# Delta rule of a hybrid block: a symmetric decay table, beta applied as the triangle leaves PSUM, key scaling in front of the weight splits, and the inverse turned over

## The chip, the cores and the metric

The kernel runs on one core of one Trainium2 chip. The metric is the device time of one execution in microseconds; lower is better. Engines are called by their names in the profile: PE is TensorE (PEld its weight loads), DVE VectorE, ACT ScalarE, POOL GpSimd, SP SyncE, which only issues transfers here. Each engine works through its own list of instructions in order, and engines wait for each other by semaphores.

## The reference

Two transformer-like blocks over 512 tokens of width 1024. The change lies in one branch of the first block, a gated delta rule with 8 heads, keys of 128 and values of 256 columns. Everything is float32.

```python
qa = l2norm(qa) * (A_DK ** -0.5)
ka = l2norm(ka)
beta = jax.nn.sigmoid(beta_logit)
g = -jnp.exp(a_log) * jax.nn.softplus(a_dt + dt_bias)
...
g_cum = jnp.cumsum(g, axis=-1)                      # within a chunk
decay = jnp.exp(jnp.where(causal, g_cum[..., :, None] - g_cum[..., None, :], -jnp.inf))
k_beta = k * beta[..., None]
lower = jnp.where(strict, jnp.einsum('bhncd,bhnmd->bhncm', k_beta, k) * decay, 0.0)
t_inv = triangular_solve(lower, eye, unit_diagonal=True)
u = t_inv @ (v * beta)
w = t_inv @ (k_beta * exp(g_cum))
attn = jnp.where(causal, jnp.einsum('bhncd,bhnmd->bhncm', q, k) * decay, 0.0)
# then chunk by chunk, with a state of 128 x 256 per head:
# v_new = u - w @ state;  o = (q * exp(g_cum)) @ state + attn @ v_new;  state = state * last_dec + k_dec.T @ v_new
```

The kernel takes chunks of 128 tokens, not of 64, which is the same function. All else of both blocks (projections, a retention branch, attention of three kinds, 16 experts) is as before.

## The kernel before

The program is written out by hand, one list per engine. A semaphore object (`Sig`) gives each step a name: `c_pe.mark(ins, "KK0.1")` counts it up, `dve.wait_ge(*c_pe("KK0.1"))` waits for it. In names, `j` is the head within a pair and `p` the pair; four pairs follow each other (`chain_a(p)`, p = 0 to 3, on every engine).

Between the steps of a pair lie weight matmuls of the projections that later pairs need. A generator `gemm` gives them in steps: one step is three matmuls of 128x512, the two-part product of `product` (L93, L94, L95), 8 steps a group, 12 groups a pair. `fill(n)` emits n of them at fixed places, with numbers from the table `FILL` (`root` 8, `scores` 6, `turn` 6, `inverse` 4, `level` 3 and 3, ...). On ScalarE and VectorE the same `fill` emits what belongs to a group that has ended: the eviction of its bank (L797), the high part of a later weight piece (L82 on ScalarE), its low part (L87 on VectorE), and the convolution of the next pair (L808, L1918, L812). A weight piece is split four groups ahead of use. SyncE loads 2 MB of weights when the group that read the slot last has ended.

The steps of a pair, in TensorE's order, with the lines of the profile:

1. Sums of squares of queries and keys by a matmul with ones (L1317 into `bank_a`, L1318 into `bank_b`, head by head), behind the scaling of the previous pair's output (L2031) that reads `bank_a`.
2. ScalarE makes 1/norm of them: a logarithm (L851), a table load, an exponential (L856, "root"), and then the exponential of the decay table D (L859), which VectorE has laid out (L1952). Then it does its `fill(root)`.
3. VectorE does its own `fill(root)` (one weight split, L87) and then scales keys (L1958) and queries (L1961).
4. GpSimd multiplies the scaled keys by beta (L590, `kbT`), masks D to a triangle (L593), and makes the queries for the state (L598, `qeT`).
5. TensorE does 8 steps of weights, then KK = keys by beta-keys (L1324) and KQ = keys by queries (L1329). VectorE multiplies both by D as they leave PSUM (L1965 into `LT`, L1968 into `ATT`).
6. After 6 steps, keys and values are transposed (L1334, L1344); GpSimd masks `LT` with the mask of level 0 (L609).
7. The inverse of I + L by 7 levels of doubling blocks. Per level: GpSimd masks (`NM`, L609), TensorE multiplies by X (L1359), ScalarE copies (L873), TensorE makes the updates of X and Y (L1367, L1370), VectorE adds them (L1997, L2000). X is the inverse and Y its transpose, weight steps lie between.
8. The recurrence over the four chunks (L1385 to L1402), norms, transposes of the output (L1410), and its scaling (L2031).

## Time and profile before

| | us |
|---|---|
| median of 3 runs | 2854.88 |
| lowest, highest | 2853.36, 2857.54 |
| the profiled execution | 2853.58 |
| its span in the profile | 2851.9 |
| PE busy | 2582.3 (91%) |
| DVE busy | 1122.2 (39%) |
| ACT busy | 833.4 (29%) |
| POOL busy | 250.7 (9%) |

The span is the time between the first and the last instruction of one execution. Busy shares are averages over the whole program. The four pairs of the delta rule lie between about 86 and 650 us of the span. A row of the timeline gives start, duration, engine, line, operation and how many instructions were merged into it; in brackets is how long the engine had stood idle and whose instruction ended that. A float32 matmul shows as two records, so 16 records are 8 products. A matmul's duration includes its way through the array, so consecutive ones overlap: work is read from starts.

### The profile page before, as it was taken

The page shows a single profiled execution, that of the slowest core. Times are in us where ns is not written, and L with a number is a line of the kernel's source. Part 1 is how long each engine was busy: PE and PEld are TensorE (multiplying, and loading weights), DVE is VectorE, ACT ScalarE, POOL GpSimd, SP SyncE. Part 2 cuts the span into 40 slices and gives each one's busy share as a digit, 9 for nine tenths or more (in the row PEclk, how much of TensorE's full clock was granted, in tenths as well). Part 3 has the DMA queues.
Part 4 walks back from the last instruction along what each step waited for, and adds up shares of the span by engine and source line. Part 5 has one row for each costly group of instructions (what it writes and reads, how often), then busy time and mean ns, then how long its engine had stood idle before and what let it go on. Part 6 is the DMA issues. An engine that isn't in the chain of part 4 may idle for free.

```text
span 2851.9 us, 30016 instructions
## 1 busy us (share of the span) xinstructions
PE 2582.3 (91%) x12308; PEld 1928.0 (68%) x12308; DVE 1122.2 (39%) x1539; ACT 833.4 (29%) x1327; POOL 250.7 (9%) x240
## 2 busy tenths in 40 slices
PE   6898989899999899988999999786999969999996
PEld 4687878787777677776778887464687754444442
DVE  4655555525233423244334452536433361111213
ACT  5434343333222313133233332434422210000000
POOL 0212121313001000000000001312000000000000
PEclk9999999999999999998999999898999979999998
DMA  4021222203222224231222234110223269999995
GB/s 152 33 68 66 70 72 60 96 30 133 93 85 104 103 89 148 89 131 69 89 89 89 96 127 144 59 41 12 100 79 113 76 250 367 409 409 409 409 409 210
DMA packets 155278, 404.68 MB, mean 142 GB/s; under 512 B 7440, under 2 KB 25232, under 8 KB 155024
## 3 DMA queue, kind: packets, MB, share of 16 engines
...
## 4 chain that ended last, share of the span: by engine, by line
PE 80%; DVE 7%; DMA 5%; ACT 4%; issue 2%; POOL 1%; SPq 0%; DVEq 0%; POOLq 0%; ACTq 0%
PE banks L93 18%; PE banks L95 17%; PE banks L94 17%; PE banks L1813 4%; PE banks L1844 4%; DMA work<-w_down_in 2%; PE banks L1794 2%; PE banks L1871 2%; PE banks L1704 2%; DMA ring<-w_down_in 2%; PE banks L1370 2%; PE banks L1679 1%; PE banks L1367 1%; PE banks L1463 1%; DVE ring_split L87 1%
## 5 line engine op out<-in xcount | busy, mean ns | idle before, releaser
L93 PE MATMUL banks<-work_split,ring_split 128*128 128x512 f32 x1536 | 619.3, 403 | 43.0 <-DVE ring_split L87 26.0
L87 DVE TENSOR_TENSOR ring_split<-ring,ring_split 128x1024 fp32r<-128x1024 f32 (+1 forms) x296 | 358.8, 1229 | 760.4 <-ACT ring_split L82 760.4
L94 PE MATMUL banks<-work_split,ring_split 128*128 128x512 f32 x1536 | 604.4, 394 | 0.0
L95 PE MATMUL banks<-activations_T_split,ring_split 128*128 128x512 f32 x1184 | 466.7, 394 | 0.0
L82 ACT ACTIVATE ring_split<-ring 128x1024 fp32r<-128x1024 f32 (+1 forms) x296 | 302.3, 1040 | 320.1 <-PE banks L95 258.0
L93 PEld LDWEIGHTS banks<-work_split,ring_split 128*128 128x128 f32 x1536 | 292.7, 191 | 108.3 <-DVE ring_split L87 30.3
L94 PEld LDWEIGHTS banks<-work_split,ring_split 128*128 128x128 f32 x1536 | 293.1, 191 | 59.6 <-issue 1.0
L94 PE MATMUL banks<-ring_split,work_split 128*128 128x512 f32 (+1 forms) x736 | 286.9, 390 | 0.0
L95 PE MATMUL banks<-ring_split,work_split 128*128 128x512 f32 (+1 forms) x736 | 286.5, 389 | 0.0
L95 PEld LDWEIGHTS banks<-activations_T_split,ring_split 128*128 128x128 f32 x1184 | 225.4, 190 | 48.4
L93 PE MATMUL banks<-ring_split,work_split 128*128 128x512 f32 x384 | 152.8, 398 | 15.1 <-DVE ring_split L87 10.0
L94 PEld LDWEIGHTS banks<-ring_split,work_split 128*128 128x128 f32 x736 | 140.7, 191 | 28.6 <-issue 0.7
L95 PEld LDWEIGHTS banks<-ring_split,work_split 128*128 128x128 f32 x736 | 140.5, 191 | 28.3
L93 PE MATMUL banks<-ring_split,activations_T_split 128*128 128x512 f32 (+1 forms) x352 | 138.5, 393 | 9.4 <-DVE ring_split L87 9.4
L95 PE MATMUL banks<-work_split,ring_split 128*128 128x512 f32 x352 | 137.9, 392 | 0.0
L1813 PE MATMUL banks<-ring,work 128*64 128x512 f32 x512 | 111.4, 593 | 0.0
L1813 PE MATMUL banks<-work 128*64 128x512 f32 x384 | 111.4, 593 | 0.0
L2458 DVE TENSOR_TENSOR work<-banks,work 128x512 f32<-128x512 f32 x64 | 44.3, 692 | 150.7 <-PE banks L1871 150.7
L797 ACT ACTIVATE work<-banks 128x512 f32<-128x512 f32 x60 | 35.8, 597 | 228.8 <-PE banks L95 211.4
L609 POOL TENSOR_TENSOR work<-work,const 128x512 f32<-128x512 f32 x56 | 83.4, 1507 | 142.8 <-PE banks L1359 105.8
L93 PEld LDWEIGHTS banks<-ring_split,work_split 128*128 128x128 f32 x384 | 73.8, 192 | 31.9 <-DVE ring_split L87 10.8
L2449 DVE TENSOR_TENSOR work<-banks,work 128x512 f32<-128x512 f32 x16 | 11.1, 692 | 209.9 <-PE banks L1813 209.9
...
## 6 DMA issues: line engine op xcount, KB each, us to landing
...
```

The costliest lines, as they stand in the source:

```text
L82: s.mark(act.activation(R(dst), src, ACT.Copy), what)
L87: s.mark(dve.tensor_tensor(R(dst), src, R(hi).bitcast(F32), ALU.subtract), what)
L93: pe.matmul(out, R(ll), R(rh), start=start, stop=False)
L94: pe.matmul(out, R(lh), R(rh), start=False, stop=False)
L95: return pe.matmul(out, R(lh), R(rl), start=False, stop=stop)
L609: c_pool.mark(pool.tensor_tensor(by_t(NM[:, j, :]), LT[j], m_lvl[:, s, :].unsqueeze(1).broadcast_to([P, NT, P]), ALU.mult), f"NM{s}_{j}.{p}")
L1370: mm = pe.matmul(bank_c[j][:, c], PP[j][:, t, :], Y[j][:, t, :], start=True, stop=True)
L1704: mm = pe.matmul(o, lhsT, pT[:, m % 2, k * P:(k + 1) * P], start=(k == 0), stop=(k == nk // P - 1))
L1794: mm = pe.matmul(psum[b // 4][:, b % 4 * P:(b % 4 + 1) * P], XR[:, t, b * P:(b + 1) * P], SP[:, t, :], start=(t == 0), stop=(t == NT - 1))
L1813: mm = pe.matmul(psum[3 + q // 2 + 2 * f][64 * e:64 * e + 64, :], xst[:, q % 2 * 4 + k, 64 * e:64 * e + 64], weights(12 * p + 2 * q + e, k ...
L1844: mm = pe.matmul(psum[4 + n][64 * e:64 * e + 64, :], actT[:, 4 * q + k, 64 * e:64 * e + 64], weights(12 * p + 8 + 2 * q + e, k, n), start= ...
L1871: e_pe.mark(pe.matmul(psum[(0, 1, 2, 6)[m % 4]][:, :], SGT[:, t * P:(t + 1) * P], ye[:, n, :], start=True, stop=True), f"y{m}.{p}")
```

## The change

- **Decay table.** `D` (masked on GpSimd, in `dl`) becomes `E` = exp(sign x distance) = exp(-|difference|), the same for a pair of tokens in either order, in the memory of `kbT`. `sign` is +1 and -1, made once on GpSimd. VectorE lays it out with one three-operand instruction per chunk instead of a tensor_scalar.
- **Beta.** KK is now keys by keys; beta comes in as a per-token scalar when VectorE takes the product out of PSUM (`L`, four instructions a head instead of one). GpSimd's `kbT` product and one of three broadcast rows per head go away.
- **Mask.** `E` isn't masked. `L` needs none beside the level masks; `ATT` is masked on GpSimd behind the level 2 masks, and TensorE waits for that before the first output.
- **Order on VectorE.** Its `fill(root)` (the weight split) stands behind L and ATT instead of in front of the key scaling.
- **Sums of squares.** Keys of both heads first, then queries; queries go to `bank_c` instead of `bank_a`, so the waits are for the previous pair's gate (keys) and for the first part of its output (queries).
- **Inverse.** `L` stands the other way round than `LT`, so X and Y change places in each level and the level masks in `constants` are turned.

The diff, with context lines left out and the indentation cut:

```diff
@@ -150,7 +150,9 @@
 u8 = dl.rearrange("p j n -> p (j n)")[:, 0:1536].rearrange("p (a n) -> p a n", a=3)
-D, LT = [[by_t(dl[:, j, at:at + 512]) for j in range(2)] for at in (0, 512)]
+E = [by_t(kbT[:, j, :]) for j in range(2)]
+L = [by_t(dl[:, j, 512:1024]) for j in range(2)]
+sign = wsm.rearrange("p k n -> p (k n)")[:, 0:P]
 oN = [by_t(dl[:, j, :]) for j in range(2)]
@@ -571,7 +573,7 @@
     pool.wait_ge(*s_dma("rows"))
-for n, r in enumerate((0, 32, 96)):
+for n, r in ((0, 0), (2, 96)):
     a_bc[j].mark(pool.dma_start(bc[:, j, n, :], scratch[h + r:h + r + 1, :].broadcast_to([P, SEQ])), f"r{n}.{p}")
@@ -582,38 +584,37 @@
 
-    for j in range(2):
-        pool.wait_ge(*a_bc[j](f"r2.{p}"))
-        pool.wait_ge(*c_vec(f"kT{j}.{p}"))
-        if p:
-            pool.wait_ge(*c_pe(f"V3_{j}.{p - 1}"))
-        c_pool.mark(pool.tensor_tensor(kbT[:, j, :], y[:, 2 + j, :], bc[:, j, 1, :], ALU.mult), f"kbT{j}.{p}")
-    for j in range(2):
-        pool.wait_ge(*c_act(f"D{j}.{p}"))
-        c_pool.mark(pool.tensor_tensor(D[j], D[j], m_incl.unsqueeze(1).broadcast_to([P, NT, P]), ALU.mult), f"D{j}.{p}")
-    for j in range(2):
-        pool.wait_ge(*c_vec(f"qT{j}.{p}"))
-        if p:
-            pool.wait_ge(*c_pe(f"O3{j}.{p - 1}"))
-        c_pool.mark(pool.tensor_tensor(qeT[:, j, :], y[:, j, :], bc[:, j, 2, :], ALU.mult), f"qeT{j}.{p}")
     for s in range(LEVELS):
...
             if s == 0:
-                pool.wait_ge(*c_vec(f"LT{j}.{p}"))
+                pool.wait_ge(*c_vec(f"L{j}.{p}"))
...
             if s == 1:
-                pool.wait_ge(*c_vec(f"Y0_{j}.{p}"))
-            c_pool.mark(pool.tensor_tensor(by_t(NM[:, j, :]), LT[j], m_lvl[:, s, :].unsqueeze(1).broadcast_to([P, NT, P]), ALU.mult),
+                pool.wait_ge(*c_vec(f"X0_{j}.{p}"))
+            c_pool.mark(pool.tensor_tensor(by_t(NM[:, j, :]), L[j], m_lvl[:, s, :].unsqueeze(1).broadcast_to([P, NT, P]), ALU.mult),
                         f"NM{s}_{j}.{p}")
+        for j in range(2):
+            if s == 0:
+                pool.wait_ge(*a_bc[j](f"r2.{p}"))
+                pool.wait_ge(*c_vec(f"qT{j}.{p}"))
+                if p:
+                    pool.wait_ge(*c_pe(f"O3{j}.{p - 1}"))
+                c_pool.mark(pool.tensor_tensor(qeT[:, j, :], y[:, j, :], bc[:, j, 2, :], ALU.mult), f"qeT{j}.{p}")
+            if s == 2:
+                pool.wait_ge(*c_vec(f"ATT{j}.{p}"))
+                c_pool.mark(pool.tensor_tensor(ATT[j], ATT[j], m_incl.unsqueeze(1).broadcast_to([P, NT, P]), ALU.mult), f"ATT{j}.{p}")
...
 
+pool.wait_ge(*ld_const("consts"))
+pool.wait_ge(*s_pe("proj"))
+z_pool.mark(pool.tensor_scalar(sign, m_incl, 2.0, -1.0, ALU.mult, ALU.add), "sign")
 for j in range(2):
@@ -845,9 +846,9 @@
 fill = over(round_of(p)[0], lambda i: after(p, i))
-for j in range(2):
-    act.wait_ge(*c_pe(f"ss{j}.{p}"))
-    for n, bank in ((1, bank_b), (0, bank_a)):
+for n, what, bank in ((1, "k", bank_b), (0, "q", bank_c)):
+    for j in range(2):
+        act.wait_ge(*c_pe(f"ss{what}{j}.{p}"))
@@ -855,8 +856,8 @@
 for j in range(2):
-    act.wait_ge(*c_vec(f"Dpre{j}.{p}"))
-    c_act.mark(act.activation(D[j], D[j], ACT.Exp), f"D{j}.{p}")
+    act.wait_ge(*c_vec(f"dist{j}.{p}"))
+    c_act.mark(act.activation(E[j], E[j], ACT.Exp), f"E{j}.{p}")
@@ -867,7 +868,7 @@
 if s > 1:
-    act.wait_ge(*c_pe(f"Y{s - 1}_{j}.{p}"))
+    act.wait_ge(*c_pe(f"X{s - 1}_{j}.{p}"))
@@ -1306,25 +1307,26 @@
 qT, kT = [[y[:, at + j, :] for j in range(2)] for at in (0, 2)]
-for j in range(2):
-    pe.wait_ge(*c_act(f"sqk{j}.{p}"))
-    if p:
-        pe.wait_ge(*c_vec(f"oT1{j}.{p - 1}"))
-    elif j == 0:
-        pe.wait_ge(*s_vec("begN"))
-        pe.wait_ge(*n_act("AT6"))
-        pe.wait_ge(*n_vec("AT7"))
-    pe.matmul(bank_a[j][:, :], ones, sq[:, j, 0, :], start=True, stop=True)
-    c_pe.mark(pe.matmul(bank_b[j][:, :], ones, sq[:, j, 1, :], start=True, stop=True), f"ss{j}.{p}")
+for n, what, bank in ((1, "k", bank_b), (0, "q", bank_c)):
+    for j in range(2):
+        pe.wait_ge(*c_act(f"sqk{j}.{p}"))
+        if p:
+            pe.wait_ge(*(c_vec(f"gate{j}.{p - 1}") if n else c_vec(f"oT0{j}.{p - 1}")))
+        elif n and j == 0:
+            pe.wait_ge(*s_vec("begN"))
+            pe.wait_ge(*n_act("AT6"))
+            pe.wait_ge(*n_vec("AT7"))
+        c_pe.mark(pe.matmul(bank[j][:, :], ones, sq[:, j, n, :], start=True, stop=True), f"ss{what}{j}.{p}")
...
     pe.wait_ge(*c_vec(f"kT{j}.{p}"))
-    pe.wait_ge(*c_pool(f"kbT{j}.{p}"))
     for c in c4:
-        mm = pe.matmul(bank_c[j][:, c], kT[j][:, c], kbT[:, j, c], start=True, stop=True)
+        mm = pe.matmul(bank_c[j][:, c], kT[j][:, c], kT[j][:, c], start=True, stop=True)
     c_pe.mark(mm, f"KK{j}.{p}")
...
     pe.wait_ge(*c_vec(f"qT{j}.{p}"))
+    if p:
+        pe.wait_ge(*c_vec(f"oT1{j}.{p - 1}"))
     for c in c4:
@@ -1335,7 +1337,7 @@
 pe.wait_ge(*c_act(f"silu{5 + 2 * j}.{p}"))
-pe.wait_ge(*c_vec(f"LT{j}.{p}"))
+pe.wait_ge(*c_vec(f"L{j}.{p}"))
 for t in range(NT):
@@ -1354,21 +1356,21 @@
 pe.wait_ge(*c_pool(f"NM{s}_{j}.{p}"))
-pe.wait_ge(*c_vec(f"X{s - 1}_{j}.{p}"))
+pe.wait_ge(*c_vec(f"Y{s - 1}_{j}.{p}"))
 for t, c in enumerate(c4):
-    mm = pe.matmul(bank_a[j][:, c], NM[:, j, c], X[j][:, t, :], start=True, stop=True)
+    mm = pe.matmul(bank_a[j][:, c], NM[:, j, c], Y[j][:, t, :], start=True, stop=True)
 c_pe.mark(mm, f"P{s}_{j}.{p}")
...
 pe.wait_ge(*c_act(f"P{s}_{j}.{p}"))
-pe.wait_ge(*c_vec(f"Y{s - 1}_{j}.{p}"))
+pe.wait_ge(*c_vec(f"X{s - 1}_{j}.{p}"))
+for t, c in enumerate(c4):
+    mm = pe.matmul(bank_c[j][:, c], X[j][:, t, :], PP[j][:, t, :], start=True, stop=True)
+c_pe.mark(mm, f"Y{s}_{j}.{p}")
...
     for t, c in enumerate(c4):
-        mm = pe.matmul(bank_b[j][:, c], Y[j][:, t, :], PP[j][:, t, :], start=True, stop=True)
+        mm = pe.matmul(bank_b[j][:, c], PP[j][:, t, :], X[j][:, t, :], start=True, stop=True)
     c_pe.mark(mm, f"X{s}_{j}.{p}")
-for t, c in enumerate(c4):
-    mm = pe.matmul(bank_c[j][:, c], PP[j][:, t, :], Y[j][:, t, :], start=True, stop=True)
-c_pe.mark(mm, f"Y{s}_{j}.{p}")
@@ -1397,6 +1399,8 @@
 pe.wait_ge(*c_act(f"vnew{t}_{j}.{p}"))
+if t == 0:
+    pe.wait_ge(*c_pool(f"ATT{j}.{p}"))
@@ -1947,12 +1951,13 @@
     if p:
-        dve.wait_ge(*c_pe(f"oT1{j}.{p - 1}"))
+        dve.wait_ge(*c_pe(f"V3_{j}.{p - 1}"))
+    elif j == 0:
+        dve.wait_ge(*z_pool("sign"))
     for t in range(NT):
-        i = dve.tensor_scalar(D[j][:, t, :], bc[:, j, 0, t * P:(t + 1) * P], stN[:, t, 2 * p + j:2 * p + j + 1], 0.0,
-                              ALU.subtract, ALU.min)
-    c_vec.mark(i, f"Dpre{j}.{p}")
-fill(FILL["root"])
+        i = dve.scalar_tensor_tensor(E[j][:, t, :], bc[:, j, 0, t * P:(t + 1) * P], stN[:, t, 2 * p + j:2 * p + j + 1], sign,
+                                     ALU.subtract, ALU.mult)
+    c_vec.mark(i, f"dist{j}.{p}")
 for j in range(2):
@@ -1961,11 +1966,15 @@
     dve.wait_ge(*c_pe(f"KK{j}.{p}"))
-    dve.wait_ge(*c_pool(f"D{j}.{p}"))
-    c_vec.mark(dve.tensor_tensor(LT[j], by_t(bank_c[j][:, :]), D[j], ALU.mult), f"LT{j}.{p}")
+    dve.wait_ge(*c_act(f"E{j}.{p}"))
+    for t in range(NT):
+        i = dve.scalar_tensor_tensor(L[j][:, t, :], bank_c[j][:, t * P:(t + 1) * P], stN[:, t, 2 * p + j + 32:2 * p + j + 33],
+                                     E[j][:, t, :], ALU.mult, ALU.mult)
+    c_vec.mark(i, f"L{j}.{p}")
 for j in range(2):
     dve.wait_ge(*c_pe(f"KQ{j}.{p}"))
-    c_vec.mark(dve.tensor_tensor(ATT[j], by_t(bank_a[j][:, :]), D[j], ALU.mult), f"ATT{j}.{p}")
+    c_vec.mark(dve.tensor_tensor(ATT[j], by_t(bank_a[j][:, :]), E[j], ALU.mult), f"ATT{j}.{p}")
+fill(FILL["root"])
@@ -1981,23 +1990,23 @@
 dve.wait_ge(*c_pool(f"NM0_{j}.{p}"))
-c_vec.mark(dve.tensor_tensor(Y[j], by_t(NM[:, j, :]), eye, ALU.add), f"Y0_{j}.{p}")
-dve.wait_ge(*c_pe(f"P0_{j}.{p}"))
...
     dve.wait_ge(*oa_st[j](f"o.{p - 1}"))
-c_vec.mark(dve.tensor_tensor(X[j], by_t(bank_b[j][:, :]), eye, ALU.add), f"X0_{j}.{p}")
+c_vec.mark(dve.tensor_tensor(X[j], by_t(NM[:, j, :]), eye, ALU.add), f"X0_{j}.{p}")
+dve.wait_ge(*c_pe(f"P0_{j}.{p}"))
+c_vec.mark(dve.tensor_tensor(Y[j], by_t(bank_b[j][:, :]), eye, ALU.add), f"Y0_{j}.{p}")
...
 for j in range(2):
+    dve.wait_ge(*c_pe(f"Y{s}_{j}.{p}"))
+    dve.wait_ge(*c_vec(f"Y{s - 1}_{j}.{p}"))
+    c_vec.mark(dve.tensor_tensor(Y[j], by_t(bank_c[j][:, :]), Y[j], ALU.add), f"Y{s}_{j}.{p}")
...
         c_vec.mark(dve.tensor_tensor(X[j], by_t(bank_b[j][:, :]), X[j], ALU.add), f"X{s}_{j}.{p}")
-    dve.wait_ge(*c_pe(f"Y{s}_{j}.{p}"))
-    dve.wait_ge(*c_vec(f"Y{s - 1}_{j}.{p}"))
-    c_vec.mark(dve.tensor_tensor(Y[j], by_t(bank_c[j][:, :]), Y[j], ALU.add), f"Y{s}_{j}.{p}")
@@ -2476,7 +2485,7 @@
 same = i[:, None] // (2 * w) == i[None, :] // (2 * w)
-lv.append(-(same & (i[:, None] // w % 2 == 0) & (i[None, :] // w % 2 == 1)).astype(float))
+lv.append(-(same & (i[:, None] // w % 2 == 1) & (i[None, :] // w % 2 == 0)).astype(float))
```

On VectorE, the head of pair 0. The first instructions lay out the decay table (L1952 before, L1958 now), `ring_split` is the weight split, `residual` holds queries and keys, `banks` are PSUM. Before:

```order
L1952 TENSOR_SCALAR work<-work 128x128 [waits a_rows0]
L1952 TENSOR_SCALAR work<-work 128x128 x3
L1952 TENSOR_SCALAR work<-work 128x128 [waits a_rows1]
L1952 TENSOR_SCALAR work<-work 128x128 x3
L87 TENSOR_TENSOR ring_split<-ring,ring_split 128x8x128 [waits a_gemm_act]
L1958 TENSOR_TENSOR residual<-residual,work 128x512 [waits a_chain_act] x2
L1961 SCALAR_TENSOR_TENSOR residual<-residual,work 128x512 [waits a_chain_act] x2
L1965 TENSOR_TENSOR work<-banks,work 128x512 [waits a_chain_pool,a_chain_pe] x2
L1968 TENSOR_TENSOR work<-banks,work 128x512 [waits a_chain_pe] x2
L1973 TENSOR_TENSOR ring<-banks,work 128x512 [waits a_chain_pe]
L1974 TENSOR_TENSOR ring<-banks,work 128x512
```

and now:

```order
L1958 SCALAR_TENSOR_TENSOR work<-work 128x128 [waits pool_setup,a_rows0]
L1958 SCALAR_TENSOR_TENSOR work<-work 128x128 x3
L1958 SCALAR_TENSOR_TENSOR work<-work 128x128 [waits a_rows1]
L1958 SCALAR_TENSOR_TENSOR work<-work 128x128 x3
L1963 TENSOR_TENSOR residual<-residual,work 128x512 [waits a_chain_act] x2
L1966 SCALAR_TENSOR_TENSOR residual<-residual,work 128x512 [waits a_chain_act] x2
L1971 SCALAR_TENSOR_TENSOR work<-banks,work 128x128 [waits a_chain_act,a_chain_pe]
L1971 SCALAR_TENSOR_TENSOR work<-banks,work 128x128 x3
L1971 SCALAR_TENSOR_TENSOR work<-banks,work 128x128 [waits a_chain_act,a_chain_pe]
L1971 SCALAR_TENSOR_TENSOR work<-banks,work 128x128 x3
L1976 TENSOR_TENSOR work<-banks,work 128x512 [waits a_chain_pe] x2
L87 TENSOR_TENSOR ring_split<-ring,ring_split 128x8x128 [waits a_gemm_act]
```

The split that stood ahead of the key scaling (L1958 before, L1963 now) stands behind the products' way out of PSUM; these are four small instructions a head for L (L1971), and wait for ScalarE instead of GpSimd.

On GpSimd, one pair (p = 1); `a_chain_...` are the steps of the other engines, `a_rows` the broadcast rows. Before:

```order
L590 TENSOR_TENSOR work<-residual,work 128x512 [waits a_chain_pe,a_chain_vec,a_rows0]
L590 TENSOR_TENSOR work<-residual,work 128x512 [waits a_chain_pe,a_chain_vec,a_rows1]
L593 TENSOR_TENSOR work<-work,const 128x512 [waits a_chain_act] x2
L598 TENSOR_TENSOR work<-residual,work 128x512 [waits a_chain_pe,a_chain_vec] x2
L609 TENSOR_TENSOR work<-work,const 128x512 [waits a_chain_pe,a_chain_vec] x2
L609 TENSOR_TENSOR work<-work,const 128x512 [waits a_chain_vec,a_chain_pe] x2
L609 TENSOR_TENSOR work<-work,const 128x512 [waits a_chain_pe] x10
```

and now:

```order
L597 TENSOR_TENSOR work<-work,const 128x512 [waits a_chain_pe,a_chain_vec] x2
L605 TENSOR_TENSOR work<-residual,work 128x512 [waits a_chain_pe,a_chain_vec,a_rows0]
L605 TENSOR_TENSOR work<-residual,work 128x512 [waits a_chain_pe,a_chain_vec,a_rows1]
L597 TENSOR_TENSOR work<-work,const 128x512 [waits a_chain_vec,a_chain_pe] x2
L597 TENSOR_TENSOR work<-work,const 128x512 [waits a_chain_pe] x2
L608 TENSOR_TENSOR work<-work,const 128x512 [waits a_chain_vec] x2
L597 TENSOR_TENSOR work<-work,const 128x512 [waits a_chain_pe] x8
```

The keys' product (L590) and the mask of D (L593) in front are gone; the level 0 mask comes first, then the queries' product (L605), and the mask of ATT (L608) lies behind level 2.

On TensorE, the head of pair 1, weight steps (L93 to L95) left out. Before:

```order
L1410 MATMUL banks<-const,work 128x128 [waits a_chain_vec]
L1410 MATMUL banks<-const,work 128x128 x7
L1317 MATMUL banks<-work,const 128x512 [waits a_chain_vec,a_chain_act]
L1318 MATMUL banks<-work,const 128x512
L1317 MATMUL banks<-work,const 128x512 [waits a_chain_vec,a_chain_act]
L1318 MATMUL banks<-work,const 128x512
L1324 MATMUL banks<-work,residual 128x128 [waits a_chain_pool,a_chain_vec]
L1324 MATMUL banks<-work,residual 128x128 x3
L1324 MATMUL banks<-work,residual 128x128 [waits a_chain_pool,a_chain_vec]
L1324 MATMUL banks<-work,residual 128x128 x3
L1329 MATMUL banks<-residual 128x128 [waits a_chain_vec]
L1329 MATMUL banks<-residual 128x128 x3
L1329 MATMUL banks<-residual 128x128 [waits a_chain_vec]
L1329 MATMUL banks<-residual 128x128 x3
```

and now:

```order
L1414 MATMUL banks<-const,work 128x128 [waits a_chain_vec]
L1414 MATMUL banks<-const,work 128x128 x7
L1414 MATMUL banks<-const,work 128x128 [waits a_chain_vec]
L1414 MATMUL banks<-const,work 128x128 x7
L1319 MATMUL banks<-work,const 128x512 [waits a_chain_vec,a_chain_act] x4
L1324 MATMUL banks<-residual 128x128 [waits a_chain_vec]
L1324 MATMUL banks<-residual 128x128 x3
L1324 MATMUL banks<-residual 128x128 [waits a_chain_vec]
L1324 MATMUL banks<-residual 128x128 x3
L1331 MATMUL banks<-residual 128x128 [waits a_chain_vec]
L1331 MATMUL banks<-residual 128x128 x3
L1331 MATMUL banks<-residual 128x128 [waits a_chain_vec]
L1331 MATMUL banks<-residual 128x128 x3
```

KK (L1324) no longer waits for GpSimd, and the sums of squares (L1319) wait each for themselves.

## Rows read from the trace of the kernel before

**Rows 1.** The page's first line.
```profile
span 2851.9 us, 30016 instructions
```

**Rows 2.** Waits of TensorE, 60 to 660 us: total, times, longest.
```profile
PE banks L1324 <- POOL work L590: 29.1, 4, 12.5
PE banks L1317 <- DVE work L2031: 7.7, 3, 2.6
```

**Rows 3.** Timeline, head of pair 0: start, us, engine, line [idle before].
```profile
86.47 1.02 PE L1317 MATMUL banks<-work,const 128*128 128x512 f32 x2
87.33 1.02 PE L1318 MATMUL banks<-work,const 128*128 128x512 f32 x2
...
95.93 2.42 ACT L851 ACTIVATE work<-banks,const 128x512 f32<-128x512 f32 x4
...
99.66 2.19 ACT L856 ACTIVATE work<-work 128x512 f32<-128x512 f32 x4
101.75 1.13 ACT L859 ACTIVATE work<-work 128x512 f32<-128x512 f32 x2
...
104.34 1.23 DVE L87 TENSOR_TENSOR ring_split<-ring,ring_split 128x1024 fp32r<-128x1024 f32 x1 [8.83 <-ACT ring_split L82]
105.49 1.29 DVE L1958 TENSOR_TENSOR residual<-residual,work 128x512 f32<-128x512 f32 x2
106.33 3.23 POOL L590 TENSOR_TENSOR work<-residual,work 128x512 f32<-128x512 f32 x2 [52.01 <-DVE residual L1958]
106.69 3.43 DVE L1961 SCALAR_TENSOR_TENSOR residual<-residual,work 128x512 f32<-128x512 f32 x2
108.04 3.75 PE L1324 MATMUL banks<-work,residual 128*128 128x128 f32 x16 [12.52 <-POOL work L590]
...
114.24 0.48 PE L93 MATMUL banks<-work_split,ring_split 128*128 128x512 f32 x1
```

**Rows 4.** Timeline, head of pair 1.
```profile
227.85 0.37 SPq L374 DMA_DIRECT2D ring<-w_in_in  x1
...
229.43 1.23 DVE L87 TENSOR_TENSOR ring_split<-ring,ring_split 128x1024 fp32r<-128x1024 f32 x1 [1.06 <-ACT ring_split L82]
230.57 2.72 DVE L2031 SCALAR_TENSOR_TENSOR work<-banks,const,work 128x512 f32<-128x512 f32 x4
232.12 1.16 PE L1317 MATMUL banks<-work,const 128*128 128x512 f32 x2 [2.56 <-DVE work L2031]
...
233.21 1.65 DVE L1952 TENSOR_SCALAR work<-work 128x128 f32<-128x128 f32 x8
...
236.93 0.80 PE L93 MATMUL banks<-work_split,ring_split 128*128 128x512 f32 x1
...
248.50 3.76 PE L1324 MATMUL banks<-work,residual 128*128 128x128 f32 x16 [5.52 <-POOL work L590]
...
254.46 0.48 PE L93 MATMUL banks<-work_split,ring_split 128*128 128x512 f32 x1
```

**Rows 5.** Windows: us, busy by engine (instructions), granted clock, DMA share, GB/s.
```profile
100.00:102.00 2.00, 0.00 (x0) 0.00 (x0) 0.00 (x0) 2.00 (x5) 0.00 (x0) 0.50 0.00 0
...
238.00:240.00 2.00, 2.00 (x10) 1.62 (x9) 0.00 (x0) 1.98 (x3) 0.00 (x0) 1.00 0.00 0
...
248.00:250.00 2.00, 1.50 (x7) 1.53 (x8) 2.00 (x2) 0.00 (x0) 2.00 (x3) 0.50 0.00 0
```

**Rows 6.** Timeline, level 2 of the inverse in pair 1.
```profile
270.15 3.50 POOL L609 TENSOR_TENSOR work<-work,const 128x512 f32<-128x512 f32 x2 [0.48 <-PE banks L1359]
...
272.45 3.34 DVE L1918 SCALAR_TENSOR_TENSOR residual<-work,const,residual 128x512 f32<-128x512 f32 x3
...
275.70 0.68 DVE L1997 TENSOR_TENSOR work<-banks,work 128x512 f32<-128x512 f32 x1
...
278.88 1.95 PE L1359 MATMUL banks<-work 128*128 128x128 f32 x16
```

**Rows 7.** Groups by form, 0 to 900 us: busy us, mean ns | idle before.
```profile
L2012 DVE SCALAR_TENSOR_TENSOR work<-work,banks 128x256 f32<-128x256 f32 x16 | 7.7, 480 | 31.9 <-PE banks L1402 31.9
```

## The prediction

> **What bounds the kernel now.** I read the page first, then the waits of TensorE over the first block's delta rule, then the timeline of all engines around those waits, then the granted clock in two-microsecond windows. The page gives a span of 2851.9 us [rows 1]; the profiled execution took 2853.58 us, so 1.7 us lie around the span, and the median of the three timed runs is 2854.88, 1.3 above the profiled one. TensorE is the engine on whose order everything hangs. From 60 to 660 us, where the four head pairs of the delta rule run between matmuls of the weight projections, it waits in few places. The reader should see two: 29.1 us in 4 waits at L1324, for GpSimd's product at L590 (the longest 12.5), and 7.7 us in 3 waits at L1317 for VectorE's L2031 (longest 2.6) [rows 2]. The change touches exactly these.
>
> Pair 0 shows the chain behind the first wait. ScalarE's logarithms start at 95.93, its four roots at 99.66 (0.55 us apart), then two exponentials of the decay at 101.75, and only behind these a PSUM eviction and a weight split. VectorE stands at its own half of that split (104.34), because it is written ahead of the key scaling (105.49). GpSimd's product of keys and beta follows (106.33), and TensorE starts KK at 108.04 after 12.52 us idle [rows 3]. So roots that are ready from 100.3 are used at 105.5. Pair 1 has the same chain with 5.52 us idle at 248.50, and an earlier gap of 2.56 us at 232.12, where the sums of squares wait for the previous pair's output to leave the banks [rows 4]. Pairs 2 and 3 repeat pair 1: 7.7 is three times 2.56, and 29.1 less 12.52 is three times 5.5 [rows 2].
>
> The idle time also costs clock. In 100 to 102 us and in 248 to 250 us the granted clock was 0.50, its 1.2 GHz level, after TensorE had been idle; in 238 to 240 us, behind busy matmuls, 1.00 [rows 5]. The price shows in the work: KK and KQ (16 products of 128 columns) took 6.20 us in pair 0 (108.04 to 114.24) [rows 3] and 5.96 us in pair 1 (248.50 to 254.46), and the four sums of squares took 4.81 us (232.12 to 236.93) [rows 4], where at full clock one starts 0.86 us after the other (86.47, 87.33) [rows 3]: 3.44 for four. A 128-column product is a quarter of that, 0.215, so KK and KQ are worth 3.44 at full clock.
>
> **The change, part by part, in pairs 1 to 3.** TensorE's transposes of the previous output end at 229.56 (232.12 less 2.56) [rows 4].
> - Sums of squares, keys first. The two key sums go to a bank whose last reader is the gate, which the transposes had to wait for as well, so they run from 229.56 to 231.3, in what was idle time. The first query sum needs only the first of the four L2031 operations (from 230.57, 0.68 apart [rows 4]): ready at 231.3. The second needs the third, ready at about 232.7, and ends at 233.6. Idle left: some 0.5 us instead of 2.56. With a gap that small I take the clock as full.
> - Eight steps of weight matmuls follow, the same as before. Before they took 6.05 us with the drain (236.93 to 242.98, which is 248.50 less 5.52 [rows 4]), the first at half clock; I take 5.5. They end at 239.1.
> - Keys. ScalarE takes its last logarithm behind the second query sum, 233.8 to 234.5, then the table load of 1.28 us (the time between the end of the logarithms and 99.66 in pair 0 is this load), then roots 0.55 apart, the first at 236.4. VectorE no longer has the split in front, so the two key scalings (1.29 us for both [rows 3]) are ready at 237.1 and 237.8. GpSimd's product, 3.23 us for two [rows 3], is gone from the path: KK takes the keys themselves. TensorE wants the first at 239.1: 2.0 us of slack, the wait is gone.
> - Queries. The two scalings took 3.43 us beside GpSimd's product [rows 3]; alone a VectorE operation of three operands and 512 columns starts every 0.68 us (the L2031 row over four) and ends within 0.75 [rows 4]. They end at about 239.3; KQ wants them at 240.8.
> - So KK and KQ run 239.1 to 242.6 at full clock. Before, they ended at 254.46. **Saved: 11.9 us a pair**, of which 2.1 are the first gap, 5.5 the second, 2.5 the clock in KK and KQ, 1.4 the clock in the sums and 0.5 the slow first weight step.
>
> In pair 0 nothing in front of the roots moves: ScalarE comes to its logarithms at 95.93 because of the activations before it, not of TensorE. The first root is there at 100.3, the first key at 101.05, KK starts at 101.1 instead of 108.04: 6.9 us. The clock stays down there (0.50 at 100 to 102 [rows 5]), so KK and KQ take about the 6.1 they took. **Saved: 7.0 us**, between 6.2 (half clock to their end, 6.9 us) and 9 (clock back within 2 us).
>
> Sum: 7.0 + 3 x 11.9 = 42.7 us, from 2853.6 to 2810.9 by the profiled execution, **2812 against the median**.
>
> Edits that I cost at nothing, with their cover:
> - L on VectorE is now eight operations of 128 columns with PSUM as source instead of two of 512. The trace has none of this kind. The nearest is L2012, the same operation at 256 columns: 480 ns [rows 7]. Eight of these are 3.8 us; at the rate of columns alone it would be 1.4. I take 2.2. From 240.1, even 3.8 ends at 244, and what needs it, the value transposes, comes after six more weight steps and the key transposes, at about 247.5. If that cover went, 1 to 2 us a pair would be late.
> - The table of distances loses tensor_scalar for a three-operand form: 1.65 us for eight at 233.21 [rows 4], perhaps 2.2 now, done at 235.5, wanted by ScalarE at 238.6.
> - VectorE's split and ScalarE's split of the next weights: ScalarE comes to its own at 239.7 instead of 243.7 and needs the load issued at 227.85 [rows 4]. The DMA share is 0.00 from 238 to 240 [rows 5], so it has landed, with 2 us to spare. ScalarE is in order, so a late load would stop all behind it; that is the new neighbour.
> - One broadcast of a row less per head, one GpSimd product less per head. The mask of the diagonal triangle on ATT moves into level 2 of the inverse, two GpSimd operations more there, and waited for first at the outputs, tens of us later. The queries' product on GpSimd now comes behind the first level mask: off the path in both.
> - The inverse turned over swaps the names of X and Y but keeps one product, one copy, two products, two additions in the same order and with the same partner waited for. Nothing.
>
> **A rule against it.** In pair 1 level 2 has GpSimd's masks at 270.15 (3.50 us for two) beside VectorE's convolution at 272.45, whose three operations took 3.34 us [rows 6] where 0.75 each would be 2.3. So they do hold each other up, by about 1.1 us. The two additional masks follow directly, into the additions at 275.70, which read PSUM. TensorE wants these at 278.88 [rows 6]. Another 1.1 us is covered: four additions from 276.8 at 0.60 end at 279.3, the first at 277.5, and the second head's product wants its own at 279.8. The Trainium skill (SBUF — State Buffer, "SBUF: two separate sides") has the pair of ports shared by VectorE and GpSimd as an exclusive lock held for a whole instruction, the loser blocked. By it the convolution could alternate with all four masks and come 2.5 us late, and the second head's additions would miss TensorE by 0.5 us: 1.5 us over the three pairs that have a convolution there, 2813.5 in all. The trace agrees with the direction of it.
>
> **Rivals.**
> 1. The gaps go, the clock does not come back: the small gaps left before the query sums are enough to drop it. For: 0.50 at 248 to 250 and in the sums, each time behind idle time [rows 5]. Against: those gaps were 2.56 us and more, and the one left is 0.5. Price: up to 1.4 in the sums and 2.5 in KK and KQ, 3.9 x 3 = 11.7: 2824. If only one of them, 2816 to 2820.
> 2. A new wait inside the chain: the load or ScalarE's order. If the next weights land after 239.7, or the roots come more than 2 us later than I have them, TensorE stops before KK again. Each us is paid about once a pair, up to the 5.5 us that the wait had, 16.5: 2829.
> 3. Larger: the clock in pair 0 also comes back early (2 us), and gaps go to nothing (0.5 a pair): 2808.5.
> 4. The saving does not reach the end. Were a later stage paced by transfers that start at a time of their own, the 42.7 us would be spent there. The expert weights come behind TensorE's own matmuls, by semaphores, so I give this little: 2850 or so, no measurable change.
> 5. Slower. The idle stretches are taken as rest that the chip's clock is paid from: TensorE, busier in this region, is granted 0.50 in stretches of the level work that now run at 1.00. It would take 86 us at half clock to eat 42.7 us, and 98 us to end slower by over 0.2%; each level period of about 10 us at half clock costs 5, so it decides from ten of the 24 periods on, and at twelve gives 2872. Against it: 238 to 240 is at 1.00 behind busy work, and the clock falls only behind idle time in every window that I read.
>
> **How the numbers follow.** Forecast as told, 70 in 100; rival 1 10; rival 2 8; rival 3 7; rival 4 3; rival 5 2. The range reaches from the larger case (2808.5, less 1.5 for the spread of runs) to the half-way of rival 1: 2807 to 2821. What can be told from no change is about 0.2%, 5.7 us. Cases 1 to 3 are all faster by far more: faster 0.95, same 0.03, slower 0.02.
>
> **What would show it.** In the new profile TensorE's waits at the KK matmuls should be one, in pair 0, of about 5.5 us, and those before the sums below 0.6 us each; the granted clock in the head of pairs 1 to 3 should be 1.00; from the first key sum to the first weight step after KQ it should take 13.1 us instead of 24.9 from the end of the transposes. GpSimd should be busy 13 us less. VectorE's query scalings should fall from 1.75 to 0.75 us each. A wait of KK on VectorE in pairs 1 to 3, an idle TensorE in front of the second level's product, or a ScalarE split that waits for a load would each make the prediction wrong in its place.

## The result, and the profile after

| | before | changed |
|---|---|---|
| median, us | 2854.12 (4 runs) | 2815.15 (4 runs) |
| the profiled execution, its span | 2853.58, 2851.9 | 2814.55, 2812.9 |

The ratio of the changed kernel to the one before is 0.9857, with a 95% interval of 0.9844 to 0.987: 39.0 us faster. 2812 was forecast, in a range from 2807 to 2821.

The waits of TensorE from 60 to 660 us in the changed kernel (line waited for: us in total, times, longest), against [rows 2]:

```profile
PE banks L1324 <- DVE residual L1963: 5.6, 1, 5.6
PE banks L1405 <- ACT work L887: 2.5, 3, 0.8
PE banks L1368 <- ACT work L874: 1.8, 3, 0.6
PE banks L1319 <- DVE work L2040: 1.2, 6, 0.2
```

Of 29.1 us in front of KK one wait in pair 0 is left; the 7.7 us in front of the sums are 1.2. The timeline of pair 0 (start, us, engine, line, [idle before]), against [rows 3]:

```profile
95.89 2.42 ACT L852 ACTIVATE work<-banks,const 128x512 f32<-128x512 f32 x4
...
99.63 2.19 ACT L857 ACTIVATE work<-work 128x512 f32<-128x512 f32 x4
100.29 1.29 DVE L1963 TENSOR_TENSOR residual<-residual,work 128x512 f32<-128x512 f32 x2 [4.28 <-ACT work L857]
101.04 3.79 PE L1324 MATMUL banks<-residual 128*128 128x128 f32 x16 [5.55 <-DVE residual L1963]
```

The keys are scaled as soon as the first root is there, and KK starts 7.0 us earlier. Pair 1, whole head, against [rows 4]:

```profile
220.35 1.91 PE L1414 MATMUL banks<-const,work 128*128 128x128 f32 x16
...
222.10 1.88 PE L1319 MATMUL banks<-work,const 128*128 128x512 f32 x4
...
223.28 2.72 DVE L2040 SCALAR_TENSOR_TENSOR work<-banks,const,work 128x512 f32<-128x512 f32 x4
...
224.17 1.10 PE L1319 MATMUL banks<-work,const 128*128 128x512 f32 x2 [0.18 <-DVE work L2040]
...
225.49 1.10 PE L1319 MATMUL banks<-work,const 128*128 128x512 f32 x2 [0.22 <-DVE work L2040]
225.91 2.18 DVE L1958 SCALAR_TENSOR_TENSOR work<-work 128x128 f32<-128x128 f32 x8
...
229.29 1.29 DVE L1963 TENSOR_TENSOR residual<-residual,work 128x512 f32<-128x512 f32 x2 [1.20 <-ACT work L857]
230.50 1.29 DVE L1966 SCALAR_TENSOR_TENSOR residual<-residual,work 128x512 f32<-128x512 f32 x2
...
231.90 1.95 PE L1324 MATMUL banks<-residual 128*128 128x128 f32 x16
...
232.99 2.16 DVE L1971 SCALAR_TENSOR_TENSOR work<-banks,work 128x128 f32<-128x128 f32 x8 [1.20 <-PE banks L1324]
233.68 1.95 PE L1331 MATMUL banks<-residual 128*128 128x128 f32 x16
```

TensorE goes from the transposes through the sums, the weight steps and KK without standing still for more than 0.22 us. The windows (busy by engine, granted clock, DMA share, GB/s) show what that does to the clock, against [rows 5]:

```profile
222.00:224.00 2.00, 1.98 (x7) 0.68 (x5) 1.86 (x3) 1.97 (x3) 0.00 (x0) 1.00 0.94 327
224.00:226.00 2.00, 1.61 (x4) 0.60 (x5) 2.00 (x5) 1.40 (x3) 0.74 (x1) 1.00 1.04 408
...
232.00:234.00 2.00, 2.00 (x20) 2.00 (x19) 1.01 (x4) 1.54 (x2) 0.00 (x0) 1.00 0.00 0
```

It is 1.00 throughout, where KK and KQ ran at 0.50 before; in pair 0, with 5.55 us idle in front, it is still 0.50 (100 to 102 us). From the end of the transposes to the first weight step behind KQ it takes 13.1 us (222.26 to 235.38) instead of 24.9. The retention stage's first product starts at 628.7 us instead of 671.1: 42.4 us. By the end of the span 39.0 us of them are there; where the other 3.4 went is asked below.

### The profile page after: what moved, and what is told of

It is laid out like the page before. It is cut to its first block, busy times and chain, and to the rows that moved or that the text cites. A ratio compares the mean times of both kernels' runs of the same rounds, so it can differ in the third digit from the quotient of the medians.

```text
span 2812.9 us, 30025 instructions
## 1 busy us (share of the span) xinstructions
PE 2573.5 (91%) x12308; PEld 1920.5 (68%) x12308; DVE 1124.9 (40%) x1563; ACT 834.8 (30%) x1327; POOL 239.7 (9%) x225
## 4 chain that ended last, share of the span: by engine, by line
PE 81%; DVE 7%; DMA 5%; ACT 3%; issue 2%; POOL 1%; SPq 0%; DVEq 0%; POOLq 0%; ACTq 0%
PE banks L93 18%; PE banks L95 18%; PE banks L94 18%; PE banks L1817 4%; PE banks L1848 4%; DMA work<-w_down_in 2%; PE banks L1798 2%; PE banks L1875 2%; PE banks L1708 2%; PE banks L1368 2%; DMA ring<-w_down_in 2%; PE banks L1683 2%; PE banks L1372 1%; PE banks L1467 1%; PE banks L1361 1%
## 5 line engine op out<-in xcount | busy, mean ns | idle before, releaser
L93 PE MATMUL banks<-work_split,ring_split 128*128 128x512 f32 x1536 | 619.0, 403 | 43.0 <-DVE ring_split L87 26.1
L95 PE MATMUL banks<-activations_T_split,ring_split 128*128 128x512 f32 x1184 | 466.8, 394 | 0.0
L93 PEld LDWEIGHTS banks<-work_split,ring_split 128*128 128x128 f32 x1536 | 292.8, 191 | 107.5 <-DVE ring_split L87 30.4
L95 PE MATMUL banks<-ring_split,work_split 128*128 128x512 f32 (+1 forms) x736 | 286.6, 389 | 0.0
L95 PEld LDWEIGHTS banks<-activations_T_split,ring_split 128*128 128x128 f32 x1184 | 225.1, 190 | 48.7
L93 PE MATMUL banks<-ring_split,work_split 128*128 128x512 f32 x384 | 153.4, 399 | 15.1 <-DVE ring_split L87 10.0
L95 PEld LDWEIGHTS banks<-ring_split,work_split 128*128 128x128 f32 x736 | 140.5, 191 | 28.7
L93 PE MATMUL banks<-ring_split,activations_T_split 128*128 128x512 f32 (+1 forms) x352 | 137.9, 392 | 9.4 <-DVE ring_split L87 9.4
L95 PE MATMUL banks<-work_split,ring_split 128*128 128x512 f32 x352 | 138.0, 392 | 0.0
L93 PEld LDWEIGHTS banks<-ring_split,work_split 128*128 128x128 f32 x384 | 74.0, 193 | 31.9 <-DVE ring_split L87 10.8
```

Source lines behind the costliest of these rows:

```text
L93: pe.matmul(out, R(ll), R(rh), start=start, stop=False)
L95: return pe.matmul(out, R(lh), R(rl), start=False, stop=stop)
```

## Experiments

Two questions. Ratios below are to the kernel before, with 95% intervals. Which part of the change brought the 42.4 us: the product taken off GpSimd, whose name stands at the wait, or the order of VectorE's list, whose split stood in front of the keys? And where did the 3.4 us go? The yardstick for the first is the start of the retention stage, which lies before the later stages can add their scatter.

**Once more, unchanged.** 

> The changed kernel once more, unaltered. It saved 42.4 us by the time the retention stage starts (its first scores matmul at 671.09 us before, 628.66 after), but only 39.0 us at the end of the span. Theory A: the 3.4 us missing are scatter of the later stages, which the change does not touch; then the start of the retention stage is again at 628.7 within 0.3 us, the shift between that point and the end differs by a few us from the first profile, and the median is 2811 to 2817. Theory B: the faster head costs the later stages something of their own; then the same 3.4 us are missing again at the same places (between 938 and 1656 us, and near 2038 us of the span before).

Median 2816.1, ratio 0.9864 (0.9848 to 0.9881). Retention starts at 628.5; the rest of the span took 2185.0 us, 2184.2 in the first profile, 2180.8 in the profile of before. Up to 2100 us of its span its matmuls start where the first profile has them; from 2305 us on they come 2.6 us later, and all but 0.7 of that is made up by the end. The start and the median are as A has them, but 0.8 us between the two profiles is less than A's few us, and some 3.4 us are missing again: this run alone speaks for B.

**The order alone.** The kernel before, with:

```diff
                     c_vec.mark(i, f"Dpre{j}.{p}")
-                fill(FILL["root"])
...
                     c_vec.mark(dve.tensor_tensor(ATT[j], by_t(bank_a[j][:, :]), D[j], ALU.mult), f"ATT{j}.{p}")
+                fill(FILL["root"])
                 fill(FILL["scores"])
```

> The kernel before with one part of the change alone: VectorE's weight split in front of the key scaling is moved behind the two products that leave PSUM. GpSimd's keys-by-beta product, the masked table and the old order of the sums stay. Theory A (the split in front was the larger part of the wait that the profile names GpSimd for): in pairs 1 to 3 the key scaling comes at about 240.8 instead of 245.95 on the clock of pair 1 before, GpSimd is done with the first product at 243.3, so TensorE waits 0.4 to 1.0 us instead of 5.5 and its clock stays up: 7 us saved a pair; pair 0 saves 5.2; 26 us in all, about 2828. Theory B (GpSimd's product is what costs, as the releaser says): the wait shrinks by less than 2 us a pair, under 10 us saved in all.

Median 2829.2, ratio 0.9911 (0.9895 to 0.9928); retention starts at 643.6, 27.5 us earlier than before. One moved line, with all of GpSimd's work in place, is two thirds of the gain. Its timeline in pair 1:

```profile
233.45 1.29 DVE L1957 TENSOR_TENSOR residual<-residual,work 128x512 f32<-128x512 f32 x2 [5.84 <-ACT work L856]
234.29 3.28 POOL L590 TENSOR_TENSOR work<-residual,work 128x512 f32<-128x512 f32 x2 [7.22 <-DVE residual L1957]
...
236.04 1.13 PE L1324 MATMUL banks<-work,residual 128*128 128x128 f32 x8 [0.40 <-POOL work L590]
...
237.72 1.13 PE L1324 MATMUL banks<-work,residual 128*128 128x128 f32 x8 [0.55 <-POOL work L590]
```

GpSimd's name still stands at the wait, but for 0.40 and 0.55 us instead of 5.52; in pair 0 it is 7.4 us instead of 12.5. Theory A.

**The order undone.** The changed kernel with `fill(FILL["root"])` on VectorE back in front of the key scaling, right behind the distances.

> The changed kernel with this one part undone: VectorE's weight split stands again in front of the key scaling; no GpSimd product. Theory A: TensorE waits for the keys in pairs 1 to 3 some 3.8 us (ScalarE's eviction and high part 1.6 us behind the exponentials, VectorE's low part 1.2, the scaling 0.65), plus up to 2.5 us of clock where the idle time brings it down; pair 0 loses 5.1 us. 21 us slower than the changed kernel (15 to 24), about 2836. Theory B: the split matters little once GpSimd is gone, under 8 us slower.

Median 2834.9, 19 us behind the changed kernel; retention starts at 649.8, 21.1 us later. The waits at KK are 21.2 us in four, the longest 10.7. Pair 1:

```profile
235.85 0.60 ACT L798 ACTIVATE work<-banks 128x512 f32<-128x512 f32 x1 [0.21 <-PE banks L95]
...
237.42 1.23 DVE L87 TENSOR_TENSOR ring_split<-ring,ring_split 128x1024 fp32r<-128x1024 f32 x1 [5.55 <-ACT ring_split L82]
238.56 1.29 DVE L1964 TENSOR_TENSOR residual<-residual,work 128x512 f32<-128x512 f32 x2
239.30 3.47 PE L1324 MATMUL banks<-residual 128*128 128x128 f32 x16 [3.49 <-DVE residual L1964]
```

VectorE stands 5.55 us at a split that nobody needs yet, with the keys behind it. 3.49 us of wait where 3.8 were expected, and KK at half clock at first (3.31 us to KQ instead of 1.78). Pair 0 waits 10.7 us instead of 5.6, the 5.1 expected. Theory A.

**The old sums.** The changed kernel with the old sums on TensorE and ScalarE:

```diff
-                for n, what, bank in ((1, "k", bank_b), (0, "q", bank_c)):
-                    for j in range(2):
-                        pe.wait_ge(*c_act(f"sqk{j}.{p}"))
-                        if p:
-                            pe.wait_ge(*(c_vec(f"gate{j}.{p - 1}") if n else c_vec(f"oT0{j}.{p - 1}")))
...
+                for j in range(2):
+                    pe.wait_ge(*c_act(f"sqk{j}.{p}"))
+                    if p:
+                        pe.wait_ge(*c_vec(f"oT1{j}.{p - 1}"))
...
+                    pe.matmul(bank_a[j][:, :], ones, sq[:, j, 0, :], start=True, stop=True)
+                    c_pe.mark(pe.matmul(bank_b[j][:, :], ones, sq[:, j, 1, :], start=True, stop=True), f"ss{j}.{p}")
```

> The changed kernel with the sums of squares as before: head by head, queries into the bank that the previous pair's output leaves last. Theory A: 2.56 us idle comes back in front of them in pairs 1 to 3, with the clock loss in the sums (1.4) and the slow first weight step (0.5), less the 0.4 us of idle that the new order still has: 4 us a pair, 12 us slower, about 2827; no wait at KK, since the roots are still 2 us early. Theory B: the key path becomes late too, since the roots start later: a second wait at KK of 1 to 2 us with its clock loss, 18 us or more slower.

Median 2822.6, some 7 us behind the changed kernel, with retention at 636.2, 7.5 later. The 2.56 us are back and no wait at KK in pairs 1 to 3, as A has it, but 12 us is too much. Here is the clock in pair 1 of this kernel:

```profile
224.00:226.00 2.00, 1.17 (x3) 0.70 (x4) 2.00 (x5) 0.00 (x0) 0.73 (x1) 0.97 1.04 406
226.00:228.00 2.00, 2.00 (x3) 0.68 (x2) 2.00 (x9) 0.42 (x1) 0.73 (x1) 0.50 1.06 406
228.00:230.00 2.00, 2.00 (x5) 0.85 (x3) 0.10 (x1) 0.85 (x2) 0.00 (x0) 0.67 1.00 408
230.00:232.00 2.00, 2.00 (x10) 1.62 (x9) 0.00 (x0) 1.74 (x3) 0.00 (x0) 1.00 0.01 4
```

It falls to 0.50 behind the 2.56 us, and the four sums take 4.80 us up to the first weight step, as before (4.81). That step comes 7.36 us behind the transposes' end, in the changed kernel 3.76: 3.6 us lost. Pair 2 of the same execution has the same wait (timeline of TensorE):

```profile
356.72 1.10 PE L1318 MATMUL banks<-work,const 128*128 128x512 f32 x2 [2.56 <-DVE work L2040]
...
359.37 1.02 PE L1319 MATMUL banks<-work,const 128*128 128x512 f32 x2
359.83 0.79 PE L93 MATMUL banks<-work_split,ring_split 128*128 128x512 f32 x1
```

Here the sums took 3.11 us, and the first weight step comes 5.67 us behind the transposes: 1.9 us lost. Pair 3 is like pair 2 (3.11 us from 486.90). So the gap itself costs 1.9 us a pair, and the clock 1.7 more in pair 1 alone: 3.6, 1.9 and 1.9 are 7.4 of the 7.5 us. The expectation charged the lost clock to every pair. That can happen too: in the kernel with the order alone the same gap of 2.56 us brought the clock down in all three pairs (the sums took 4.73, 4.60 and 4.66 us).

**GpSimd kept.** The kernel before with both orders (the diffs of the two sections above, the second the other way round), and with GpSimd's product, masked table and old inverse.

> The kernel before with two parts of the change: VectorE's split behind the products, and the new order and banks of the sums. GpSimd's keys-by-beta product, the masked table, LT and the inverse as before. Theory A (the product costs next to nothing once the keys come in time): pair 0 waits 1.8 us more than the changed kernel, pairs 1 to 3 0.6 us each, since the second head's product is ready 0.6 us late; retention starts at 632 us and the median is 2819, 3.5 us behind the changed kernel. Theory B (taking GpSimd off the path is the core of the change): at least 10 us behind it.

Median 2817.8, ratio 0.9865 (0.9848 to 0.9882); retention at 632.34, 3.7 us behind the changed kernel (628.66). The waits for GpSimd's product are 9.0 us in 4, the longest 7.4. So the whole rewriting of the table, beta and the inverse is worth 3.7 us at that mark once the orders are right, some 2 in the medians. Theory A.

**Beta alone.** The changed kernel with both orders undone.

> The changed kernel with both orders undone (VectorE's split in front of the key scaling, sums head by head as before): only the symmetric table, beta on the way out of PSUM and the turned inverse are left of the change. Theory A: KK starts one GpSimd product earlier than before, 1.8 us a pair: 7 us saved against the kernel before by the time of the retention stage, about 2848. Theory B (the releaser's name is the price): most of the 29.1 us of waits that the profile gives to GpSimd goes, 20 us or more saved.

Median 2848.0 (10 runs), ratio 0.9971 (0.996 to 0.9981); retention at 661.1, 10.0 us earlier than before. Taking away the very product that the profile names for 29.1 us gives 7 by the medians. Most of the wait is still there and is now booked on VectorE:

```profile
PE banks L1324 <- DVE residual L1964: 21.8, 4, 10.7
```

That is 3.7 us in each of pairs 1 to 3 where it was 5.5. Theory A. The waits are 7.3 us shorter, which is what it expected; the mark gained 10.0 in this execution. A part of the rest is clock: from KK to the weight step behind KQ it took 6.44, 5.22 and 4.96 us in the three pairs, in pair 1 before 5.96. One profile doesn't show whether the clock does so each time; the ten times of this kernel reach from 2841.2 to 2852.0.

| kernel | start of retention, us | gained, us |
|---|---|---|
| before | 671.1 | |
| beta, table, inverse alone | 661.1 | 10.0 |
| order of the split alone | 643.6 | 27.5 |
| beta and sums (split ahead) | 649.8 | 21.3 |
| beta and split (old sums) | 636.2 | 34.9 |
| split and sums (GpSimd kept) | 632.3 | 38.8 |
| all | 628.7 | 42.4 |

What a part is worth depends on what is there already: the split's place 27.5 us as the first part and 21.1 as the last, beta, table and inverse 10.0 and 3.7, the sums 11.3 behind the split's move (643.6 to 632.3) and 7.5 as the last.

**Shifted by 1.7 us.** The changed kernel with one line: `for c in c4 * (3 if p == 3 else 1)` around the key transposes, which writes the same values three times.

> The changed kernel, with the eight key transposes of pair 3 done three times over (same result): TensorE gets 1.74 us of additional work at about 497 us, and nothing else changes. The stretch from the start of the retention stage to the end of the span was 2180.8 us before and 2184.2 and 2185.0 in the two profiles of the changed kernel. Theory A: whether a wait of TensorE of some 2.5 us in the later stages costs clock depends on when it comes, so a mere shift redistributes that: retention starts at 630.4, the stretch behind it comes out 1 to 4 us off 2184.6 in either direction, and the granted clock behind the 2.5 us wait at 1042 may be 1.00 this time. Theory B: the later stages cost 3.4 us more because of what the change does; then the stretch stays within 0.8 us of 2184.6.

Retention at 630.5; from there to the end 2180.8 us, 3.4 and 4.2 less than in the two profiles of the kernel without the shift. The wait of 2.5 us named in the expectation, in the changed kernel:

```profile
1042.01 0.80 PE L93 MATMUL banks<-work_split,ring_split 128*128 128x512 f32 x1 [2.47 <-DVE ring_split L87]
1042.60 0.63 PE L94 MATMUL banks<-work_split,ring_split 128*128 128x512 f32 x1
1043.03 0.63 PE L95 MATMUL banks<-activations_T_split,ring_split 128*128 128x512 f32 x1
```

and in the shifted one:

```profile
1043.56 0.50 PE L93 MATMUL banks<-work_split,ring_split 128*128 128x512 f32 x1 [2.46 <-DVE ring_split L87]
```

The same wait, 2.47 and 2.46 us, with the weight matmuls behind it 0.43 us apart in one case; in the other the granted clock of 1044 to 1046 us is 1.00. The medians do not show it, though: 2815.6 (2812.8 to 2821.7) against 2815.2 and 2816.1.

**Second profiles**, of the kernel before and of the shifted kernel, both unchanged.

> The kernel before, unaltered, for a second profile. In the first one the stretch from the start of the retention stage to the end of the span took 2180.8 us, the least of all beside the shifted kernel. Its executions scatter from 2849.9 to 2859.6 us. Theory A (whether a wait in the later stages costs clock is settled anew in each execution, by when it comes): the stretch differs from 2180.8 by 1 to 5 us in this profile, while the delta stage ends within 0.5 us of where it did. Theory B (it belongs to the program): 2180.8 again within 0.8.

> The shifted kernel, unaltered, for a second profile. In the first, the stretch behind the start of the retention stage took 2180.8 us, with the granted clock at 1.00 behind the 2.46 us wait at 1043.56. Theory A (settled anew in each execution): another stretch, 1 to 5 us off, since its four times reach from 2812.8 to 2821.7. Theory B (it belongs to the program): 2180.8 within 0.8 and again no loss behind that wait.

Before: span 2858.1, the same waits (29.1 and 7.7 us), retention at 671.8, and 2186.3 us from there instead of 2180.8. Shifted: span 2814.6, retention at 631.3, 2183.3 us instead of 2180.8, and this time the wait of 2.47 us at 1045.93 did cost clock:

```profile
1044.00:1046.00 2.00, 0.07 (x1) 0.08 (x1) 1.54 (x3) 2.00 (x3) 0.00 (x0) 0.94 1.04 347
1046.00:1048.00 2.00, 2.00 (x5) 1.61 (x6) 2.00 (x2) 1.46 (x2) 0.00 (x0) 0.50 1.01 392
```

One program, two executions, the same wait, 2.4 us later in the second, and the clock stays once and goes once. The stretch behind the start of retention took from 2180.8 to 2187.1 us over the profiles of all kernels, in which the code from there on is alike. Theory A, for both, with two sizes missed in the kernel before: 5.5 us of difference where 1 to 5 were expected, and a start of retention 0.7 us later where 0.5 was the limit. Its 5.5 us did not come from the wait of 2.46 us near 1084 us, which kept its clock both times, but from other places behind 1489 us. So a difference of 3.4 us between single profiles is within what one kernel shows, and need not be the change's. The averages leave a part open: all 28 times of the kernel before average 2855.5 us, the eight of the changed kernel 2815.4, which is 40.1 less, where the marks of two profiles each are 42.4 to 43.3 apart. Whether the change costs the later stages some 2 us on average is not shown.

**Pair 0 reordered.** On top of the changed kernel:

```diff
-                if i >= 2:
+                if 2 <= i < 7:
                     silu(0, i - 2)
...
                     c_act.mark(act.activation(E[j], E[j], ACT.Exp), f"E{j}.{p}")
+                if p == 0:
+                    for b in (5, 6, 7):
+                        silu(0, b)
...
-            for b in (6, 7):
-                silu(0, b)
```

and on VectorE the distances behind the key and query scaling where p is 0.

> On top of the changed kernel: in pair 0 alone ScalarE takes the last three value activations (blocks 5 to 7) behind the roots and the decay exponentials instead of in front, and VectorE lays out the decay distances behind the key and query scaling. Theory A: the roots are ready at about 94.4 instead of 100.3, the keys at 95.1, before TensorE is through its eight weight steps at 95.5, so the last large wait at KK (5.5 us) goes and KK and KQ run at full clock (2.6 us): 8 us less by the start of the retention stage, at 620.6; median 2807, give or take 3 us of the later stages. Theory B: the additional table load and the late value activations stop TensorE at the value transposes instead (they want all of it by 104), and under 4 us are left.

Median 2807.5 (5 runs), ratio 0.9835 (0.9821 to 0.985); the fastest version here. Its timeline:

```profile
94.70 2.19 ACT L857 ACTIVATE work<-work 128x512 f32<-128x512 f32 x4
95.37 1.30 DVE L1968 TENSOR_TENSOR residual<-residual,work 128x512 f32<-128x512 f32 x2 [0.59 <-ACT work L857]
96.19 1.97 PE L1325 MATMUL banks<-residual 128*128 128x128 f32 x16
```

The wait at KK is gone and KQ starts 1.8 us behind KK instead of 3.6. At the retention stage (622.7 us) 6.0 us are left of the 8: this execution reached the sums 0.9 us later than the other did (87.31 against 86.44), and two new waits, 1.6 us in all, came at the first level (L1362):

```profile
105.08 2.13 DVE L87 TENSOR_TENSOR ring_split<-ring,ring_split 128x1024 fp32r<-128x1024 f32 x1 [1.85 <-ACT ring_split L82]
...
113.06 0.68 DVE L2002 TENSOR_TENSOR work<-work,const 128x512 f32<-128x512 f32 x1
...
115.20 1.16 PE L1362 MATMUL banks<-work 128*128 128x128 f32 x8 [0.79 <-POOL work L597]
```

They name GpSimd's mask, which had to wait for VectorE's X0 (L2002). VectorE worked from 105.08 us to there without a pause, behind a weight split that it had waited for: ScalarE's part of it came after the late value activations. The median fits the 2807 expected partly by chance, since the stretch behind the mark took 2182.5 us, 1.7 and 2.5 less than in the two profiles of the changed kernel. Theory A, with 2 us less at the mark.

## Why the prediction was right

- **Bound and chain.** Right: the list in front of KK, not the engines' load. The prediction said that the roots lay 5.2 us unused behind VectorE's split, and the order alone and its undoing show that split at 27.5 us as the first part taken and 21.1 as the last.
- **The sum.** 42.7 us forecast, 42.4 at the start of retention in the first profile. Pairs 1 to 3: 11.9 each forecast; the sums of pair 2 start 128.3 us behind those of pair 1 (352.46 and 224.17) where it was 140.0 (372.07 and 232.12), which is 11.7. Pair 0: 7.0 forecast; the first weight step behind KQ came at 114.24 before and comes at 107.26 now, 7.0.
- **Sums of squares and weight steps.** Waits of 0.18 and 0.22 us where "some 0.5" stood. From the end of the transposes to the first weight step it took 3.8 us (222.26 to 226.02), forecast 4.0, and from there to KK 5.9 (to 231.90), forecast 5.5: two small errors that cancel, 9.6 us against 9.5. The 1.9 us of clock before KK were likewise split wrongly: from the first sum to the first weight step it is 3.03 us at full clock (86.44 to 89.47), not 3.44, so the clock had cost 1.8 in the sums and 0.2 in the weight steps, not 1.4 and 0.5.
- **Keys and queries.** First key ready at 229.95, wanted at 231.90: 2.0 us of slack, as worked out. Queries scaled in 0.68 us apiece without GpSimd beside them. GpSimd is busy 11.0 us less (239.7 instead of 250.7), forecast 13.
- **Edits at nothing.** L took 2.16 us for eight (2.2 forecast), the distances 2.18 (2.2 forecast), both covered.
- **The rule against it.** Level 2 of pair 1, against [rows 6]:

```profile
251.06 3.51 POOL L597 TENSOR_TENSOR work<-work,const 128x512 f32<-128x512 f32 x2 [0.49 <-PE banks L1361]
...
253.35 5.12 DVE L1922 SCALAR_TENSOR_TENSOR residual<-work,const,residual 128x512 f32<-128x512 f32 x3
...
254.53 3.39 POOL L608 TENSOR_TENSOR work<-work,const 128x512 f32<-128x512 f32 x2
...
258.39 0.68 DVE L2005 TENSOR_TENSOR work<-banks,work 128x512 f32<-128x512 f32 x1
...
259.81 1.95 PE L1361 MATMUL banks<-work 128*128 128x128 f32 x16
```

  The convolution grew from 3.34 to 5.12 us, 1.8 more, half-way between the 1.1 that I carried over from the row and the 2.5 of the lock. The size was off, the cover held: 9.88 us from one level's product to the next, against 9.86. Operations of 0.75 us came to 1.7 each beside GpSimd's. The Trainium skill (SBUF — State Buffer, "SBUF: two separate sides") has the ports that the two engines share locked for a whole instruction of either. The trace agrees in direction: by full turns with GpSimd's products of 1.28 us each operation would have taken 2.0 (an estimate from these rows).
- **The end.** The forecast took the gain through unchanged; 39.0 arrived in the medians and in the first pair of profiles, so the median is 3 us above the 2812 forecast. What it did not allow for is the scatter of the later stages, shown above at up to 6.3 us between profiles; single executions of the kernel before lie between 2849.9 and 2859.7. That 42.4 at the mark and 40.1 at the end by the averages differ for a reason of the change is neither shown nor excluded.
- **Rivals.** Rival 1 (clock stays down) did not come in pairs 1 to 3; its clock mechanism is what the windows of the kernel with the old sums show in pair 1, where the gap is back. Rival 3 did not come either: in pair 0 KK and KQ took 6.22 us (101.04 to 107.26), at half clock like before. Of rivals 2, 4 and 5 nothing was found: no wait of KK in pairs 1 to 3, most of the gain at the end, the granted clock at 1.00 in the heads. The upper end of the range, 2821, is not half-way to rival 1, as the prediction says; that would be 2818.
